# A 31-tap causal depthwise convolution taken off TensorE: four channel tiles by ScalarE products and GpSimd adds, four by VectorE taps from PSUM

## The reference

```python
def causal_dwconv(x, w, b):
    """Depthwise causal conv over positions. x (B,L,C), w (K,C), b (C). Output t reads x[t-K+1..t]."""
...
def conformer_conv(h, pw1_w, pw1_b, dw_w, dw_b, ln_g, ln_b, pw2_w, pw2_b):
    u = h @ pw1_w + pw1_b
    a, gt = jnp.split(u, 2, axis=-1)
    c = causal_dwconv(a * jax.nn.sigmoid(gt), dw_w, dw_b)
    c = jax.nn.silu(layernorm(c, ln_g, ln_b))
    return c @ pw2_w + pw2_b
```

## Time and profile before

| what | value |
|---|---|
| median of three runs | 3290.82 us (3289.83 to 3291.72) |
| the profiled execution's own time | 3290.29 us |
| its span, from first to last instruction | 3288.4 us |
| PE busy | 3215.1 us, 98% of the span |
| DVE busy | 864.1 us, 26% |
| ACT busy | 654.4 us, 20% |
| POOL busy | 245.5 us, 7% |
| chain that ended last | PE 85%, DMA 10%, DVE 4%, ACT 1%, issue 1% |
| mean granted TensorE clock | 0.995 |

### The profile page before, as it was taken

The page is one execution under the profiler, slowest core; times in us unless marked ns, Lnnn a source line. Parts: engine busy times, 40 slices in busy tenths (PEclk is TensorE's granted clock), DMA queues, the critical chain, the costliest instruction groups (busy, mean ns, idle before and its releaser), DMA issues.

```text
span 3288.4 us, 38822 instructions
## 1 busy us (share of the span) xinstructions
PE 3215.1 (98%) x15862; PEld 2437.2 (74%) x15862; DVE 864.1 (26%) x1873; ACT 654.4 (20%) x1160; POOL 245.5 (7%) x203
## 2 busy tenths in 40 slices
PE   8999999999999999999999999999999999999998
PEld 7888888888888888888788888788655544454444
DVE  4532132194232143002330024441211111111111
ACT  3531122112221043001211023340111111111111
POOL 0110010000000110100111011210000000000000
PEclk9999999999999999999999999999999999999999
DMA  5233343432243433444334434225699999999996
GB/s 223 101 128 141 128 142 141 166 115 103 115 156 128 165 129 115 154 144 151 125 139 141 154 118 179 83 103 205 256 428 428 428 429 428 428 429 428 428 428 265
DMA packets 71222, 714.93 MB, mean 217 GB/s; under 512 B 7968, under 2 KB 7968, under 8 KB 9152
## 3 DMA queue, kind: packets, MB, share of 16 engines
q1 hardware_dynamic: 70416, 710.06, 54.6%
q0 software_dynamic: 688, 3.15, 0.3%
HBM read 712.13 MB, written 1.05 MB: 217 GB/s over the span
## 4 chain that ended last, share of the span: by engine, by line
PE 85%; DMA 10%; DVE 4%; ACT 1%; issue 1%; POOL 0%; SPq 0%; DVEq 0%; ACTq 0%
PE bank L265 50%; PE bank L3011 10%; DMA weight_ring<-in_experts 9%; PE bank L284 8%; PE bank L3042 4%; PE bank L2996 2%; PE bank L2988 2%; PE bank L2236 1%; PE bank L1441 1%; DVE residual L1099 1%; PE bank L1205 0%; PE bank L1185 0%; PE bank L738 0%; PE bank L467 0%; PE bank L324 0%
## 5 line engine op out<-in xcount | busy, mean ns | idle before, releaser
L265 PE MATMUL bank<-normed_residual,weight_ring 128*128 128x256 f32 x4192 | 919.3, 380 | 0.0
L265 PEld LDWEIGHTS bank<-normed_residual,weight_ring 128*128 128x128 f32 x4192 | 792.7, 190 | 113.8 <-issue 8.5
L265 PE MATMUL bank<-arena,weight_ring 128*128 128x256 f32 x2920 | 641.4, 382 | 4.7 <-ACT arena L1493 3.9
L265 PEld LDWEIGHTS bank<-arena,weight_ring 128*128 128x128 f32 x2920 | 558.4, 192 | 82.7 <-issue 4.8
L3011 PE MATMUL bank<-weight_ring,arena 128*64 128x512 f32 x1024 | 227.8, 593 | 3.3 <-DMA weight_ring<-in_experts 3.1
L3011 PE MATMUL bank<-arena 128*64 128x512 f32 x1024 | 226.9, 596 | 2.3 <-DVE arena L3089 2.3
L284 PE MATMUL bank<-gained_residual,weight_ring 128*128 128x256 f32 x896 | 204.9, 389 | 23.7 <-DVE gained_residual L358 12.0
L3042 PE MATMUL bank<-weight_ring,arena 128*64 128x512 f32 x992 | 219.7, 595 | 0.0
L284 PEld LDWEIGHTS bank<-gained_residual,weight_ring 128*128 128x128 f32 x896 | 174.3, 195 | 51.0 <-DVE gained_residual L358 14.0
L3011 PEld LDWEIGHTS bank<-weight_ring,arena 128*64 128x64 f32 x1024 | 72.6, 137 | 153.1 <-issue 138.7
L3011 PEld LDWEIGHTS bank<-arena 128*64 128x64 f32 x1024 | 74.0, 138 | 149.3 <-issue 149.3
(11 more groups left out here) (380 smaller groups left out, 2489.2 us busy)
## 6 DMA issues: line engine op xcount, KB each, us to landing
weight_ring<-in_stream SPq DMA_DIRECT2D x290, 1024.0 KB, 4.8
weight_ring<-in_experts SPq DMA_DIRECT2D x126, 2048.0 KB, 18.6
arena<-in_experts SPq DMA_DIRECT2D x66, 2048.0 KB, 19.1
residual<-in_x SPq DMA_DIRECT2D x1, 1024.0 KB, 4.8
arena<-in_mem POOLq DMA_DIRECT2D x1, 1024.0 KB, 5.1
out<-gained_residual SPq DMA_DIRECT2D x4, 256.0 KB, 2.4
constants<-in_con SPq DMA_DIRECT2D x1, 612.5 KB, 7.1
vectors<-in_vec SPq DMA_DIRECT2D x1, 548.5 KB, 6.0
```

The lines of the kernel that those rows point to most:

```text
L265: mm = nc.tensor.matmul(PB[b][:, m * T:m * T + T], l, r, start=(kc == 0), stop=(kc == chunks - 1))
```

## The change

Tiles 0, 1, 4 and 5 (`POOL_PAIRS`, pairs 0 and 2) are computed by ACT and POOL: for each pair and each tap, ACT writes two scaled and shifted tiles into one of four product buffers (`conv_products_act`), and POOL adds both tiles to the pair's sum with one TENSOR_TENSOR (`conv_adds_pool`). Tiles 2, 3, 6 and 7 (`DVE_PAIRS`, pairs 1 and 3) stay with DVE's taps, with their input now written by the gated product into PSUM banks 4 and 5 (`conv_in`). The diagonal matrices, their 62 products on PE and the copy of their sums go. The newest tap with the bias is written by ACT for all four pairs. The mean takes the tiles in the order 0 to 7. The 60 product steps are spread by hand over ACT's queue.

```diff
--- before.py
+++ after.py
@@ -1156,6 +1156,7 @@
 
         def conf_pool(pool, own):
             sums_pool(pool, own, "b1_1_in")
+            conv_adds_pool(pool)
             sums_pool(pool, own, "b1_1_mix")
 
 
@@ -1281,7 +1282,7 @@
 
 
         FF, UG, UV = 0, 22, 26
-        CB0 = {0: 12, 1: 35}
+        CB0 = {0: 12, 1: 34}
 
         def branch(base, q):
             return lambda j: A[:, base + 2 * (q % 2) + j, :]
@@ -1337,13 +1338,7 @@
                     wait_conv(act, l, p - 1)
                     u = A[:, UG + 2 * (q % 2):UG + 2 * (q % 2) + 2, :]
                     nc.scalar.activation(u, u, ACT.Silu).then_inc(sem["sg_ready"], 1)
-            if l == 0:
-                act.wait_ge(sem["ff_ready"], 11)
-                for t in range(2):
-                    for k in range(CF_K):
-                        ins = nc.scalar.activation(diag(t, k), ident, ACT.Identity, scale=vec("dw_w", k * 8 + 6 + t))
-                ins.then_inc(sem["conv_base"], 1)
-            else:
+            if l == 1:
                 tables_act(act, 0)
                 act.wait_ge(sem["lam_mm"], 1)
                 nc.scalar.activation(LAME, PB[6][:, 0:8], ACT.Exp).then_inc(sem["lam_exp"], 1)
@@ -1408,15 +1403,8 @@
         CIN, CV, SIG, SWEPT1 = 0, 8, 16, 84
         cvt = tiles(CV)
         MEAN = A[:, 20, :]
-        CONV_Q = 3
-        CONV_PART = 13
-
-        def diag(t, k):
-
-            at = (22 if t == 0 else 38) + k // 2
-            if at >= 48:
-                at += 8
-            return A[:, at, k % 2 * P:k % 2 * P + P]
+        POOL_PAIRS, DVE_PAIRS = (0, 2), (1, 3)
+        TAPS, PRODS, CPROD = CF_K - 1, 4, 22
 
         def pw1_swept(p):
             return A[:, SWEPT1 + 2 * p:SWEPT1 + 2 * p + 2, :]
@@ -1434,21 +1422,14 @@
                 for m in range(2):
                     half_pe(pe, "pw1", p, m, ht, ready=h_after("b1_1_in") if p == 2 else None)
             memory_pe(pe, "xa_k1", 2)
-            wait_glu(pe, 3)
-            pe.wait_ge(sem["conv_base"], CB0[1])
-            for j in range(2):
-                for s in range(CF_K):
-                    mm = nc.tensor.matmul(PB[4][:, j * T + s:j * T + T], diag(j, CF_K - 1 - s), A[:, CIN + 6 + j, 0:T - s],
-                                          start=(s == 0), stop=(s == CF_K - 1))
-            mm.then_inc(sem["conv_mm"], 1)
             memory_pe(pe, "xa_k1", 3)
             memory_pe(pe, "xa_v1", 0)
-            for n, t in enumerate((6, 7, 0, 1, 2, 3, 4, 5)):
-                if t >= 6:
-                    pe.wait_ge(sem["conv_out"], 1)
+            for t in range(8):
+                if t // 2 in POOL_PAIRS:
+                    pe.wait_ge(sem["conv_out"], TAPS * (POOL_PAIRS.index(t // 2) + 1))
                 else:
-                    pe.wait_ge(sem["cv_ready"], t // 2 + 1)
-                mm = nc.tensor.matmul(PB[6][:, 0:T], ones, cvt(t), start=(n == 0), stop=(n == 7))
+                    pe.wait_ge(sem["cv_ready"], DVE_PAIRS.index(t // 2) + 1)
+                mm = nc.tensor.matmul(PB[6][:, 0:T], ones, cvt(t), start=(t == 0), stop=(t == 7))
             mm.then_inc(sem["mean_mm"], 1)
             memory_pe(pe, "xa_v1", 1)
             norm_pe(pe, "ln")
@@ -1457,7 +1438,7 @@
         def conf_base_act(act, q):
             wait_glu(act, q)
             for j in range(2):
-                ins = nc.scalar.activation(cvt(2 * q + j), A[:, CIN + 2 * q + j, :], ACT.Identity,
+                ins = nc.scalar.activation(cvt(2 * q + j), conv_in(2 * q + j), ACT.Identity,
                                            bias=vec("dw_b", 2 * q + j), scale=vec("dw_w", (CF_K - 1) * 8 + 2 * q + j))
             ins.then_inc(sem["cv_base"], 1)
 
@@ -1477,15 +1458,18 @@
                     ins = nc.scalar.activation(A[:, SIG + 2 * (q % 2) + j, :], src[:, j, :], ACT.Sigmoid,
                                                bias=vec("pw1_b", 8 + 2 * q + j))
                 ins.then_inc(evac[b] if q else sem["swept_gate"], 1)
-                if q < CONV_Q:
+                if q < 3:
                     conf_base_act(act, q)
+                if q:
+                    conv_products_act(act, 10 * q - 10, 10 * q)
+            conf_base_act(act, 3)
+            conv_products_act(act, 30, 40)
             memory_copy_act(act, "xa_k1", 2)
-            act.wait_ge(sem["conv_mm"], 1)
-            for j in range(2):
-                ins = nc.scalar.activation(cvt(6 + j), PB[4][:, j * T:j * T + T], ACT.Identity, bias=vec("dw_b", 6 + j))
-            ins.then_inc(sem["conv_out"], 1)
+            conv_products_act(act, 40, 46)
             memory_copy_act(act, "xa_k1", 3)
+            conv_products_act(act, 46, 52)
             memory_copy_act(act, "xa_v1", 0)
+            conv_products_act(act, 52, 60)
             norm_act(act, "ln", cvt, lambda e, t: e.wait_ge(sem["centered"], t // 4 + 1))
             memory_copy_act(act, "xa_v1", 1)
             for t in range(8):
@@ -1506,29 +1490,62 @@
                 b = wait_pair(dve, "pw1", 2 * q + 1)
                 src = bank(b)
             for j in range(2):
-                ins = nc.vector.scalar_tensor_tensor(out=A[:, CIN + 2 * q + j, :], in0=src[:, j, :],
+                ins = nc.vector.scalar_tensor_tensor(out=conv_in(2 * q + j), in0=src[:, j, :],
                                                      scalar=vec("pw1_b", 2 * q + j),
                                                      in1=A[:, SIG + 2 * (q % 2) + j, :], op0=ALU.add, op1=ALU.mult)
             ins.then_inc(evac[b] if q else sem["swept_conv"], 1)
 
-        def conv_taps_dve(dve, own, lo, hi):
-
-            taps = CF_K - 1
+        def conv_in(t):
+            q, m = t // 2, t % 2
+            if q in DVE_PAIRS:
+                return PB[4 + DVE_PAIRS.index(q)][:, m * T:m * T + T]
+            return A[:, CIN + t, :]
+
+        def prod(n):
+            return A[:, CPROD + 2 * (n % PRODS):CPROD + 2 * (n % PRODS) + 2, :]
+
+        def conv_products_act(act, lo, hi):
+
             for n in range(lo, hi):
-                q, s = n // taps, n % taps + 1
+                q, s = POOL_PAIRS[n // TAPS], n % TAPS + 1
+                if n == TAPS:
+                    wait_glu(act, q)
+                if n >= PRODS:
+                    act.wait_ge(sem["conv_out"], n - PRODS + 1)
+                for j in range(2):
+                    t = 2 * q + j
+                    ins = nc.scalar.activation(prod(n)[:, j, s:T], A[:, CIN + t, 0:T - s], ACT.Identity,
+                                               scale=vec("dw_w", (TAPS - s) * 8 + t))
+                ins.then_inc(sem["conv_mm"], 1)
+
+        def conv_adds_pool(pool):
+
+            for n in range(2 * TAPS):
+                q, s = POOL_PAIRS[n // TAPS], n % TAPS + 1
+                if s == 1:
+                    pool.wait_ge(sem["cv_base"], q + 1)
+                if n:
+                    pool.wait_ge(sem["conv_out"], n)
+                pool.wait_ge(sem["conv_mm"], n + 1)
+                c = A[:, CV + 2 * q:CV + 2 * q + 2, s:T]
+                nc.gpsimd.tensor_tensor(c, c, prod(n)[:, :, s:T], ALU.add).then_inc(sem["conv_out"], 1)
+
+        def conv_taps_dve(dve, own, n, lo, hi):
+
+            q = DVE_PAIRS[n]
+            for s in range(lo, hi):
                 if s == 1:
                     wait_glu(dve, q)
                     dve.wait_ge(sem["cv_base"], q + 1)
                 else:
                     own.wait()
-                for j in range(2):
-                    t = 2 * q + j
+                for t in (2 * q, 2 * q + 1):
                     ins = nc.vector.scalar_tensor_tensor(
-                        out=cvt(t)[:, s:T], in0=A[:, CIN + t, 0:T - s], scalar=vec("dw_w", (CF_K - 1 - s) * 8 + t),
+                        out=cvt(t)[:, s:T], in0=conv_in(t)[:, 0:T - s], scalar=vec("dw_w", (TAPS - s) * 8 + t),
                         in1=cvt(t)[:, s:T], op0=ALU.mult, op1=ALU.add)
-                    if s < taps:
+                    if s < TAPS:
                         own(ins)
-                if s == taps:
+                if s == TAPS:
                     ins.then_inc(sem["cv_ready"], 1)
 
         def conf_dve(dve, own):
@@ -1537,7 +1554,10 @@
                 scaled_dve(dve, "pw1", p, pw1_swept(p))
             for q in range(4):
                 glu_dve(dve, q)
-                conv_taps_dve(dve, own, CONV_PART * q, CONV_PART * q + CONV_PART if q < 3 else CONV_Q * (CF_K - 1))
+                if 1 <= q < 3:
+                    conv_taps_dve(dve, own, 0, 13 * q - 12, 13 * q + 1)
+            conv_taps_dve(dve, own, 0, 27, TAPS + 1)
+            conv_taps_dve(dve, own, 1, 1, TAPS + 1)
             dve.wait_ge(sem["mean_mm"], 1)
             own(nc.vector.tensor_scalar(MEAN, PB[6][:, 0:T], 1.0 / D, None, ALU.mult))
             own.wait()
```

## The result

The changed kernel takes 3297.86 us (median of 19 runs, 3296.68 to 3300.00) where the kernel before takes 3290.91 (19 runs beside it). The ratio is 1.0022, with a 95% interval of 1.0014 to 1.0029: slower by 7 us. The forecast was 3300.3 with a range from 3295 to 3311. The profiled execution took 3297.79 us, its span 3296.0 beside 3288.4.

A forecast was written before the change was run, and what follows sets the result against it. PE and DVE were taken to be in balance before the mean; afterwards POOL's add chain sets the end. Variance 7.1 us later plus 2.4 of clock loss on 3290.3, plus 0.5 for the median: 3300.3 us, range 3295 to 3311.

The forecast's parts named there:

- What goes: PE's 62 diagonal products, 25.2 us, leave its queue; dropping ACT's diagonal building and copy of the sums gains nothing.
- The start of the chain: ACT issues product 0 behind pair 1's newest tap, which waits for pw1 pair 3; first product at 678.9 us.
- The adds: POOL's sixty dependent adds at 1.315 us, 78.9 us plus 0.3 for a late ACT, ending at 758.1 us.
- the hop from one add to the next: Distance between POOL's dependent adds beyond their duration, part of the 1.285 to 1.345 us cadence.
- Contention: DVE's taps beside POOL's adds: with one input in a PSUM bank they don't lock each other out; no cost.
- Rival (c): Contention if a tap's SBUF scale counts as second input: 26 us more on POOL's adds, 3326 us; 10% with weaker forms.
- DVE's end: DVE's 60 steps of 0.88 us end at 742, 16 us inside POOL's chain, at no cost; next thing late.
- The clock: PE's lower clock behind its 32 us wait in the mean costs 2.4 us, the middle of 1.7 and 3.1.
- counted in both kernels: The half clock at 768 us, behind PE's 3.9 us wait, stays in both kernels and adds nothing.
- Sum: Whole program: 7.1 + 2.4 = +9.5 us on 3290.3, giving 3299.8; with 0.5 for the median, 3300.3 us.
- (a): POOL adds at the pace of its squares, 1.08 us; 3289 us, not slower; decides from 1.11 us downwards; 5%.
- (b): No hop between POOL's adds, 1.205 us each: chain ends at 751.5, shift 2.9 us, 3294 us; 11%.

The follow-up runs named there:

- e2: Changed kernel with the inputs of pairs 1 and 3 written to SBUF instead of PSUM banks, so DVE's taps read two SBUF tensors; 3328.01 us, one run.
- e5: Changed kernel without the 30 product steps and 30 adds of pair 2, so it doesn't compute the convolution; 3281.52 us, one run.
- e4: Changed kernel with two POOL sums per pair, joined at the end, so each add waits for the one before the last; 3295.49 us, ratio 1.0015.
- e1: Changed kernel with ACT's products moved ahead of its other work, the first right behind pair 0's newest tap; 3285.16 us, ratio 0.9981.
- e6: Changed kernel with tile 5 as 31 diagonal products on PE, ACT and POOL keeping tiles 0, 1, 4, products started early; 3278.52 us, ratio 0.9963.

## Why the prediction was right

The sign, the mechanism and the place came out as written, and the number was 2.4 us high on the median: 1.9 of them stand in the sum below, and the rest is the 0.5 us that was added for the median, which lay 0.07 us above the profiled execution this time.

- **What goes, 25.2 us off PE.** PE was through with xa_v1's first pair and half the mean at 725.8, forecast 725.7.
- **The start of the chain.** First add at 678.73, forecast 678.9. ACT's product steps took 0.90 us, forecast 0.95.
- **The adds: the term that was mis-sized.** The sum took 1.315 us an add, the middle of 1.285 and 1.345. With the one gap they took 77.60 us, forecast 79.2. The lengths were right (median 1.208 us, forecast 1.205); the hop from one add to the next was 0.07 to 0.08 us, the lower bound, and not 0.11. The last add ended at 756.33, forecast 758.1. These are 1.8 us of the total, 1.6 for the adds and 0.2 for their start. The bound from the earlier trace rows was met, the wider hop of the earlier trace rows was not, and the middle between them was a choice without a reason of its own.
- **Contention, costed at nothing.** The taps took 0.44 us, and the adds ran at the length of undisturbed ones. e2 shows what the banks avoid. Rival (c) asked 26 us for contention, put on POOL's adds; where contention does happen (e2) the loss is 30 us, near that, but on DVE's taps, at 1.29 us each beside the adds, and DVE ends last.
- **DVE's end.** 741.1, forecast 742; e5 confirms that it is next.
- **The clock.** Forecast 2.4 us behind the wait, measured 2.5. That it came so close is partly luck: 2.4 was the middle of 1.7 and 3.1 without a reason of its own, and waits of other lengths lost anything from 1.7 to 3.1 (last section). Behind the next wait "counted in both kernels" held: the windows of 0.85 and 0.72 lose 4 x 0.15 + 4 x 0.28 = 1.7 us of clock, as the one of 0.57 did before, and the 112 matmuls took 26.01 us where they took 26.10. The shift fell from 7.86 us at the variance to 7.76 behind these matmuls and to 7.6 at the end; the last 0.15 us are not traced.
- **Sum.** Forecast +9.5 on the profiled execution; -1.8 for the adds and their start, +0.1 for the clock behind the wait, -0.1 for the next wait and some -0.15 that is not traced make +7.6, which is the span's 3296.0 - 3288.4.
- **Rivals (a) and (b)** needed adds of 1.11 us, or 1.205 from start to start. Adds in place took neither here; e4 came to 1.16 by taking the dependence out.

That the change is slower says nothing against its parts. It takes 25 us from an engine that was just in balance with DVE and gives POOL a chain that ends 7 us too late. With the chain begun when its data is there (e1) it gains 6 us, and with half of the products left on PE (e6) 12.

## What to carry to other kernels

Before work is moved off a bound engine, write down for each receiver when its first input is there, its step times its count, and so its end; the move gains only as much as the latest of these ends before the donor's old one. Look first for an earlier start of that chain, then for a split that fills the donor's wait. A gain that is proved at its place and missing in the total has to be followed along the span to where it is lost.

## What the runs showed of the hardware that was not expected

- Eight unread matmuls more, 2500 us earlier, went with a wait for issue of 2.7 to 3.0 us in the program's last mean, and with the low clock behind it 4.4 us were lost there (3.0 us ahead on arrival, 1.4 behind on leaving); the medians are 3299.99 and 3295.14 us. A comparison at the 0.1% level between kernels of different length can carry such a wait.
- Under contention in e2 DVE paid and POOL hardly: taps of 0.44 us came to 1.29 beside the adds, adds from 1.28 to 1.34 us from start to start. In the earlier trace rows it was the other way round: there the eight DVE instructions took 3.25 us, as eight of the same form do with POOL idle (e6, at 754.25 us), and the one POOL sum took 2.66 us in place of 1.27. DVE read two SBUF inputs in both; what decides who pays was not tried.
- Adds that don't wait for the one just before (e4) started 1.16 us apart though each was recorded as 1.21 us long: on POOL the records of neighbouring instructions overlap, and start-to-start is the number to cost with.
- The clock loss did not follow the length of the wait: 1.7 us lost behind 3.90 us of waiting, 3.1 behind 12.10 (e2: 796.54 - 785.63 = 10.91, less the 7.8 of two tiles and the pair), 1.7 behind 14.46 (e5: 752.86 - 743.39 = 9.47, less 7.8), 2.2 behind 17.38 (e1: 755.00 - 744.21 = 10.79, less 8.6), 2.5 behind 30.56.
